# A hybrid scan and retrieval backbone: the adaLN modulation products dealt out anew over the stages

## The reference, cut to what matters

```python
silu_c, silu_cc = silu(c), silu(c_ctx)
for l in range(2):
    mod   = silu_c  @ w_mod[l] + b_mod[l]        # 6*1024 columns: sh1 sc1 g1 sh2 sc2 g2
    mod_c = silu_cc @ w_mod[l] + b_mod[l]
    proj  = (x * (1 + sc1) + sh1) @ w_in[l]      # scan input, z, pool, two gates
    y     = bidirectional_ssd(conv(proj))        # chunks of 128 tokens, 16 heads, 4 groups
    yg    = (y + d_skip * xh) * silu(z)
    yg    = yg * rsqrt(mean(yg * yg, over each of 4 groups) + eps)
    mix   = (sig(gp) * pool(proj) + sig(gs) * (yg * norm_g @ w_ssd_out)) @ w_o
    x     = layer_norm(ALPHA * x + g1 * mix)
    x     = layer_norm(ALPHA * x + g2 * peer(x * (1 + sc2) + sh2))
```

## Time and profile before

| | us |
|---|---|
| median of 3 runs (lowest, highest) | 4852.55 (4849.31, 4854.78) |
| the profiled execution's own time | 4852.04 |
| its span in the trace | 4850.2 |

### The profile page before, as it was taken

The page is one execution under the profiler, slowest core; times in us unless marked ns, Lnnn a source line. Parts: engine busy times, 40 slices in busy tenths (PEclk is TensorE's granted clock), DMA queues, the critical chain, the costliest instruction groups (busy, mean ns, idle before and its releaser), DMA issues. The chain is left out here.

```text
span 4850.2 us, 47618 instructions
## 1 busy us (share of the span) xinstructions
PE 3440.4 (71%) x15218; PEld 1720.0 (35%) x15218; DVE 3190.4 (66%) x6620; ACT 1537.8 (32%) x3751; POOL 2027.4 (42%) x1553
## 2 busy tenths in 40 slices
PE   7788889896778976555555557889897555555555
PEld 5576324332367433111111115777742111111111
DVE  5365787664465668776777756584566777777775
ACT  3442344343262235222222214362222222222221
POOL 0063444452023444555555550013345555555554
PEclk9889999998779998777777778979998777777777
DMA  5546999998633999999999991232299999999998
GB/s 198 207 144 260 410 418 410 423 423 365 255 115 128 380 418 401 403 420 417 411 417 422 415 418 51 81 103 78 104 374 407 418 413 420 413 412 419 416 416 362
DMA packets 263605, 1596.67 MB, mean 329 GB/s; under 512 B 43885, under 2 KB 50861, under 8 KB 77357
## 3 DMA queue, kind: packets, MB, share of 16 engines
q0 software_dynamic: 184320, 1342.26, 66.8%
q1 hardware_dynamic: 77738, 248.58, 14.2%
q10 hardware_dynamic: 1296, 2.79, 0.2%
HBM read 1575.86 MB, written 17.66 MB: 329 GB/s over the span
## 5 line engine op out<-in xcount | busy, mean ns | idle before, releaser
L2470 PE MATMUL banks<-arena 128*64 128x512 f32 x5120 | 1594.2, 759 | 1105.7 <-ACT arena L2293 1104.9
L2077 POOL DMA_INDIRECT arena<-in_experts,arena x1280 | 1497.9, 1170 | 1637.4 <-PE banks L2470 1375.7
L2163 DVE CUSTOM_DVE_ANT_0 arena<-arena,token_copies 128x1024 f32<-128x1024 f32 x1280 | 1637.0, 1297 | 669.0 <-DMA arena<-in_experts,arena 605.1
L2470 PEld LDWEIGHTS banks<-arena 128*64 128x64 f32 x5120 | 384.5, 166 | 2156.3 <-ACT arena L2293 1537.1
L2286 ACT ACTIVATE arena<-arena 128x2 f32<-128x2 f32 x640 | 131.2, 205 | 1776.7 <-DVE arena L2163 1767.4
L2293 ACT ACTIVATE arena<-arena 128x64 f32<-128x64 f32 x1280 | 376.0, 340 | 284.3 <-POOL arena L1948 243.7
L287 POOL TENSOR_TENSOR wide_low<-wide_blocks,wide_high 128x1024 fp32r<-128x1024 f32 x86 | 218.0, 2556 | 348.4 <-ACT wide_high L276 348.4
L924 POOL TENSOR_TENSOR arena<-arena 128x1024 f32<-128x1024 f32 x20 | 40.6, 2055 | 669.7 <-POOLq L807 610.0
L2349 PE MATMUL banks<-arena,wide_blocks 128*128 128x512 f32 (+3 forms) x960 | 311.7, 474 | 8.2 <-ACT arena L2192 6.7
L325 PE MATMUL banks<-activation_a,wide_high 128*128 128x512 f32 (+1 forms) x768 | 276.0, 359 | 8.4 <-ACT arena L349 2.7
L2422 PE MATMUL banks<-arena,wide_blocks 128*128 128x512 f32 x576 | 275.0, 615 | 0.0
(11 more groups left out here) (257 smaller groups left out, 4690.1 us busy)
## 6 DMA issues: line engine op xcount, KB each, us to landing
wide_blocks<-in_wide SPq DMA_DIRECT2D x168, 1024.0 KB
arena<-cum_rows SPq DMA_DIRECT2D x80, 256.0 KB, 3.2
arena<-in_experts,arena POOLq DMA_INDIRECT x1280
pre_scan<-arena SPq DMA_DIRECT2D x16, 256.0 KB
arena<-pre_scan SPq DMA_DIRECT2D x16, 256.0 KB, 9.3
residual<-in_tokens SPq DMA_DIRECT2D x6, 512.0 KB
arena<-mod_rows SPq DMA_DIRECT2D x6, 512.0 KB
norm_rows<-in_keys SPq DMA_DIRECT2D x3, 1024.0 KB
```

What stands on the lines that cost most here:

```text
L2077: pool.indirect_dma_start(out=v.ring[:, g % RING], out_offset=None, in_=io["experts"], in_offset=bass.IndirectOffsetOnAxis(ap=c.idx[:, u % ...
L2163: last = nc.vector.tensor_tensor_reduce(out=u_row, in0=u_row, in1=k.copies[:, n % NJ], scale=1.0, scalar=0.0, op0=ALU.mult, op1=ALU.add, a ...
L2470: mm = nc.tensor.matmul(k.ps[j * QUAD:(j + 1) * QUAD, a + half], v.lhs[:, g % 4, j], v.ring[:, (g * NJ + j) % RING, D + half * BANK:D + (h ...
```

## The change

- `stage_mods` computes its eight blocks by `more_mods`, in strips, with ACT as mover and the bias in PE's `combine`. It waits for the small tensor `pick` and one bias row first. It loads two of the six token tiles; the other four are loaded by the context's `stage_project`.
- `stage_states` for the context takes 12 blocks instead of 16; `stage_reload` takes none instead of 8; `stage_states` for the latent tokens of layer 0 takes 8 instead of 16, one behind each step instead of three. Its end doesn't wait for the stored rows.
- `stage_outputs` takes the other 20: 4 for the context, 8 and 8 for the latent tokens. One bank (7) serves them; every fourth unit PE combines the block before and multiplies the next; DVE moves parts and rows. SP loads a wide block before every fourth row from unit 12 on, loads three more after the last row, stores the mod rows and waits for them.
- The squared sums stay in `stage_outputs` only for the latent tokens of layer 0, and come two units later there. In the two other cases they move into `stage_merge`, behind the copies of the pool inputs; the square root follows them, and DVE's normalization moves behind the pooling.
- `stage_project` no longer rounds and cuts the merge's first block in layer 1; the merge does.

```diff
@@ stage_mods
+    mods = more_mods(k, 0, 0, brow, parts, 0, 1, n_blk)
...
-            load_wides(k, sp, WIDE_SLOTS)
-            for row in range(2):
-                sp.dma_start(brow[row:row + 1], io["b_mod"][:, 0, 0:2 * D]).then_inc(k.bias_loaded.sem, 16)
+            load_wides(k, sp, 2)
+            sp.dma_start(k.pick[:], io["pick"]).then_inc(k.bias_loaded.sem, 16)
+            mods.load(sp, 0)
+            load_wides(k, sp, n_blk)
...
-            for t in range(6):
-                load_wides(k, sp, WIDE_SLOTS + t)
+            for t in range(2):
                 sp.dma_start(k.res[:, t], io["tokens"][t]).then_inc(k.loaded.sem, 16)
             load_wides(k, sp, n_blk + WIDE_SLOTS)
-            sp.wait_ge(k.mod_used.sem, n_blk)
-            sp.dma_start(io["mods"][0, :, 0:2 * D], brow[0:2]).then_inc(k.mods_stored.sem, 16)
...
+            mods.keep(sp, 0)
+            mods.done(sp)
...
@@ more_mods
+    bank = (lambda i: 7) if alone else (lambda i: 6 + i % 2)
...
+        if alone and i >= 1:
+            pe.wait_ge(k.mod_used.sem, used0 + i)
@@ stage_project
-    last_cut = n_wide - 1 if layer == 0 else n_wide
+    last_cut = n_wide - 1
...
+            load_wides(k, sp, w0 + 6)
+            if stream == CONTEXT:
+                for t in range(2, 6):
+                    sp.dma_start(k.res[:, t], io["tokens"][t]).then_inc(k.late_tokens.sem, 16)
@@ stage_states
-                mods.done(sp)
...
-                for i in range(2 + 3 * n, 5 + 3 * n if n < len(steps) - 1 else mods.count + 1) if mods else ():
+                for i in range(2 + each * n, 2 + each * (n + 1) if n < len(steps) - 1 else mods.count + 1) if mods else ():
                     mods.multiply(pe, i)
@@ stage_outputs
+    turns = {4 * i: i for i in range(count)}
+    turns[len(units) - 1] = count
...
+            mods.load(sp, 0)
             for n, (t, d, g) in enumerate(units):
+                if n >= 12 and n % 4 == 0:
+                    load_wides(k, sp, w0 + n // 4 - 2 + WIDE_SLOTS)
...
+            load_wides(k, sp, w0 + count + WIDE_SLOTS)
+            mods.keep(sp, 0)
+            mods.done(sp)
...
+                if n in turns:
+                    i = turns[n]
+                    if i >= 1:
+                        mods.combine(pe, i - 1)
+                    mods.multiply(pe, i)
+                    if i == count:
+                        finish_used(k, pe)
                 intra(n)
...
-                if (d, g) == (1, 1) and t >= 1:
+                if squares_here and (d, g) == (1, GROUPS - 1) and t >= 1:
                     squares(t - 1)
-            squares(NT - 1)
+            if squares_here:
+                squares(NT - 1)
...
+                if n in turns and turns[n] >= 1:
+                    i = turns[n]
+                    mods.move(dve, nc.vector.tensor_copy, i - 1)
+                    if i >= 2:
+                        mods.copy_out(dve, nc.vector.tensor_copy, i - 2)
...
+            mods.copy_out(dve, nc.vector.tensor_copy, count - 1)
             add_y(NT - 1)
             gate(NT - 1)
@@ stage_merge
                 nc.scalar.copy(mixed[:, g, 0:T], k.ps[:, g % 2, 0:T]).then_inc(k.pin_copied.sem, 1)
+                if g < NT:
+                    squares(g)
+            nc.scalar.activation(rms[:, 0:NT], v.e32[:, 0:NT, 0:GROUPS], ACT.Sqrt, bias=k.eps[:],
+                                 scale=1.0 / GW).then_inc(k.rms_ready.sem, 1)
@@ build
-        w = stage_states(k, 0, CONTEXT, w)
-        stage_outputs(k, CONTEXT)
+        w = stage_states(k, 0, CONTEXT, w, mod_layer=0, first=8, count=12)
+        w = stage_outputs(k, CONTEXT, False, w, 0, 20, 4)
...
-        w = stage_reload(k, 0, w)
-        w = stage_states(k, 1, LATENT, w)
-        stage_outputs(k, LATENT)
+        stage_reload(k, 0)
+        w = stage_states(k, 0, LATENT, w, mod_layer=1, first=0, count=8)
+        w = stage_outputs(k, LATENT, True, w, 1, 8, 8)
...
-        stage_outputs(k, LATENT)
+        w = stage_outputs(k, LATENT, False, w, 1, 16, 8)
```

More of the change, by code:

```diff
@@ L393, in _ @@
             nc.scalar.activation(k.csil[:, :, 0:2], cvec, ACT.Silu).then_inc(k.h_ready.sem, 1)
+            for i in range(mods.count + 1):
+                mods.take(act, i)
         @block.gpsimd
@@ L787, in decay_steps, with stage_states @@
     return s
-def stage_states(k, layer, stream, w0=None, rows=True):
+def stage_states(k, layer, stream, w0=None, rows=True, mod_layer=0, first=0, count=0):
     nc, io = k.nc, k.io
@@ L804, in stage_states @@
              if ctx or o < NT - 1]
-    mods = more_mods(k, layer, 8, k.gates[:].rearrange("p a c -> p (a c)"), v.scr[:, 3 * D:3 * D + 512], w0, 1, 16) if w0 is not None else None
+    mods = more_mods(k, mod_layer, first, k.gates[:].rearrange("p a c -> p (a c)"), v.scr[:, 3 * D:3 * D + 512], w0, 1, count) if count else None
+    each = 3 if ctx else 1
     with nc.Block() as block:
@@ L1234, in _, with squares @@
         def _(act):
-            nc.scalar.activation(rms[:, 0:NT], v.e32[:, 0:NT, 0:GROUPS], ACT.Sqrt, bias=k.eps[:],
-                                 scale=1.0 / GW).then_inc(k.rms_ready.sem, 1)
+            def squares(t):
+                for g in range(GROUPS):
+                    nc.scalar.activation(sig[:, 0, 0:GW], v.zs[:, t, g * GW:(g + 1) * GW], ACT.Square,
+                                         accum_out=v.e32[:, t, g:g + 1])
+                    act.drain()
             round_wides(k, act, w0)
@@ L1390, in stage_merge, with stage_reload @@
     return w0 + n_wide
-def stage_reload(k, layer, w0):
+def stage_reload(k, layer):
     nc, io = k.nc, k.io
@@ L1436, in store @@
                 sp.dma_start(io["pre_part"][m], part[:, m % 2]).then_inc(k.part_kept[m % 2].sem, 16)
-            load_wides(k, sp, w0 + 6)
-            store(0)
-            store(1)
-            load_wides(k, sp, w0 + mods.count)
-            store(2)
-            store(3)
-            load_wides(k, sp, w0 + mods.count + WIDE_SLOTS)
-            mods.keep(sp, 0)
-            for m in range(4, 8):
+            for m in range(8):
                 store(m)
-            mods.done(sp)
             sp.wait_ge(k.reloaded[2].sem, C + 16 * (B_TILES + 8))
@@ L1500, in _ @@
             decay.logs(act)
-            for i in range(mods.count + 1):
-                mods.take(act, i)
-                if i == 5:
-                    decay.decays(act)
+            decay.decays(act)
         @block.vector
```

99 lines of the change are left out of this document (42 added, 57 removed).

## The result

The changed kernel takes 4802.85 us (median of 4 runs, 4801.87 to 4810.33) against 4852.47 (4849.31 to 4854.78): a ratio of 0.9901, 95% interval 0.9886 to 0.9917. Two repeats, each against new runs of the kernel before, gave 0.9908 (0.9892 to 0.9925) and 0.9911 (0.9896 to 0.9925). The profiled execution of the result is the 4810.33, the slowest of the four; its span is 4808.5.

| stage | before | forecast | after | repeats |
|---|---|---|---|---|
| first | 44.4 | 36 | 39.5 | 41.0, 39.3 |
| context: projection | 100.1 | no change | 98.4 | 99.2, 98.2 |
| context: states | 54.9 | 39 | 40.7 | 38.9, 40.7 |
| context: outputs | 47.7 | 46 | 55.1 | 55.2, 55.5 |
| context: merge | 143.8 | 146 | 143.4 | 142.8, 143.2 |

What follows compares the result with a forecast made beforehand. DMA was taken to bound the states stages with modulation blocks, PE the first stage, and PE, DVE and ACT together the outputs. Terms -8 - 15.8 - 9 - 31 + 7 + 3 = -53.8 from 4852.04 gave 4798 us, range 4783 to 4818.

Steps and rivals of the forecast that it cites:

- First stage, -8: First stage: falls from 44.36 to 36 us with blocks in strips; bounds -12 and 0.
- the rival of the slow short pieces: First stage and outputs: PE falls to its lower clock between short pieces, 4806 to 4816 us; chance 0.26.
- Context's states, -15.8: Context's states: four blocks fewer, 11.0 us, and no wait for the store's landing, about 4.8; range -14 to -16.5.
- Reload, -9: Reload: without blocks, DVE's waits for PE shrink from 11.8 to 2.5 us; bounds -6 and -11.
- Layer 0's states, -31: Latent tokens' states, layer 0: 32.3 us against 63.34, six steps of PE at 3.86; bounds -33.5 and -27.
- The +2 for a low clock at the start: Layer 0's states: 2 us added to 30.3 because PE's clock is low at the stage's start.
- Outputs, +7: Three outputs stages: layer 1 +3.5, layer 0 +5, context -1.5 with bounds -4 and +4.
- my signs: Outputs: lengths near 46, 90 and 90, PE's clock above 0.72; wrong if it falls below or a stage grows over 12.
- Merges, +3: Merges: context's +2 from normalization behind the pooling, layer 1's +1; bounds 0 and +8 for both.
- The tail of the outputs: End of outputs stages: waiting for the mod rows' store leaves about 2.5 us open, hidden behind the last squares in layer 0.
- that of PE's lower clock: First stage and outputs: short pieces run at PE's lower clock, giving 4806 to 4816 us; chance 0.26.
- the one in which the outputs cover everything: Three outputs stages: shrink by 4 + 1 + 4 us instead of growing by 7, giving 4782; chance 0.22.

Runs made afterwards that it cites:

- early: Changed kernel with two loads behind the first rows, first incoming-state products before unit 0 in all outputs, first stage's store ahead of its last load: 4801.18 us.
- best: As early, but incoming-state products come before the first unit only in the context's outputs: 4798.27 us.
- fill_rows: Changed kernel with late loads, early store, ACT moving parts and rows, and useless products filling PE's gaps in the context's outputs: 4799.25 us.

## Why the prediction was right, and where its steps were not

The forecast of 4798 was 4.9 us under the median of 4802.85, inside its range, and faster came out. That it came so close is partly luck: steps that gave too little and too much made up for each other, and the profile that is read below is the slowest run, 12 us above the forecast. Step by step:

- **First stage, -8: measured -3.3 to -5.1.** PE starts at 9.2, and the last five blocks come 2.8 us apart, both as reckoned. (The terms of the sum give 35.1, not 35.2.) Two terms failed. The first three blocks took 8.1 us, not 6: PE waited 0.54 us before the third and the fourth, for ACT's copy. And the store and its landing cost 7.5 us, not 5.1:

```profile
31.95 0.29 SPq L440 DMA_DIRECT2D mod_rows<-arena  x1
39.49 0.38 SPq L558 DMA_DIRECT2D arena<-mod_rows  x1
```

It stands behind the last 1 MB loads. The store ahead of the last of them, in `early`, shows that at most 1 us is to be had from its place in the queue, counted over this stage and the next. In the repeat with 41.0 PE waited 2.12 us for the last block, and its clock then fell, so that the last combination took 1.01 us a half instead of 0.59. The row was stored 3.8 us later than in the result and the stage ended 1.5 later; the rival of the slow short pieces has a part in that, and no run tells how much.
- **Context's states, -15.8: -14.2, -16.0, -14.2.** (179.4 + 3.4 + 0.3 + 0.4 is 183.5, 0.1 less than it says.) But the 4.8 us of landing counted as free were partly passed on: the wait at the end had also let the loads ahead land, and without it the next stage's first row stands behind them.
- **Reload, -9: -9.2 to -10.4.** DVE's wait for PE before its eight products is 2.5 us in the changed kernel, the 2.5 reckoned, and the wait before the sums' copy is gone.
- **Layer 0's states, -31: -32.9 to -33.0.** The step of PE is 3.86 us as reckoned: L876 at 1247.94, 1251.80, 1255.65, 1259.51. The +2 for a low clock at the start wasn't needed.
- **Outputs, +7: measured +16.7 in the result, +11.0 and +12.0 in the repeats.** Layer 1's: -0.2 to -0.9 where +3.5 was taken and -4 to +9 allowed. There the clock rose to 0.90 and PE's short pieces filled waits; of the 6.7 us that DVE got, its idle time took all. Each copy took 0.42 and 0.40 us, as costed (0.424 and 0.41). Layer 0's: +4.5 twice, +10.0 once, for +5. The **context's: +7.3 where -1.5 was taken and +4 was the bound**, and this is the step that failed. The runs split it: 2.5 are the late first row (55.1 to 52.6), 3.4 to 3.6 are the low clock (52.1 or 52.4 to 48.75; the same order in `early` and `best` differs by 4.1), and 2.7 remain to the 46 forecast. Of these, 2.2 can be seen at the end, in `fill_rows` as in the result, where the last combination stands ahead of the last head products at 0.50. No run takes it away.

```profile
226.61 1.01 PE L467 MATMUL banks<-arena,pick_stream 128*2 128x256 f32 x2
227.55 1.01 PE L468 MATMUL banks<-pooled_gates,ones 1*2 1x256 f32 x2
228.82 1.94 PE L963 MATMUL banks<-arena 128*128 128x64 f32 x8 [0.26 <-issue]
```

  The forecast said that ACT paces this stage. It nearly did before, with PE gapless beside it at 0.50 for its first units; with one block more in that stretch PE does, until its clock rises. Of my signs, a mean clock under 0.72 was reached here (0.71), and not in the latent stages (0.81, 0.90). For this stage it was a bad sign, since the clock was 0.64 before the change.
- **Merges, +3: -0.4 and +0.9.** The first L1376 comes 54.5 us after the merge's start, where the old L1341 came after 53.7: the normalization now stands in front of it, but by the second one DVE waits for PE again, and PE waits as long for these products as before (2.5 and 1.1 us in all):

```profile
281.94 6.30 DVE L1372 TENSOR_TENSOR arena<-arena 128x1024 f32<-128x1024 f32 x2
288.17 0.47 DVE L1376 SCALAR_TENSOR_TENSOR arena<-banks,arena 128x256 f32<-128x256 f32 x1
289.70 0.48 DVE L1376 SCALAR_TENSOR_TENSOR arena<-banks,arena 128x256 f32<-128x256 f32 x1 [1.07 <-PE banks L1225]
```

- **The tail of the outputs** was put at 2.5 us open; in the two stages without squares it is 0.3 and 0.7. In layer 1 the gate ends at 3191.8 (3190.53 + 1.23) and the next stage begins at 3192.47.

The terms in the result's own profile add up to -45.2 against -53.8: states and reload 1.7 better, first stage 3.1 worse, outputs 9.7 worse, merges 2.5 better. The rest, from -45.2 to the -41.7 of the spans, lies in stages that were put at nothing, 4.6 of it in the expert stages. Of the rivals, that of PE's lower clock came true in one stage of those it named, and now and then in part of another; the one in which the outputs cover everything came true in layer 1. As the two pull against each other, the forecast stood between them.

The Trainium skill (TensorE: Matmul & The Clock Gate, the section on HAM oscillation) says that PE loses its full rate in a loop whose wait for data is longer than the work between two waits. The context's outputs agree: their clock fell to 0.50 in a wait of 8.6 us behind 2 us of work. The first stage is another case, with waits of 0.5 to 1.0 us between pieces of about 2, and there the clock stayed at 1.00 from 10 to 30 us; the forecast's rival took the page too widely when it put the strips there at half rate.

## What to carry to other kernels

A wait at the end of a stage that looks like waste may be the time in which loads ahead land; when it goes, put the loads that the next stage needs first at the head of the queue, and the ones for later behind them. Work that is "hidden beside other engines" has its price at the clock that PE has just then: where a short stage opens with a wait of several us, as here, reckon its first units at the low clock. And look for the low clock in the instructions' own lengths, since no wait is noted for it.

## What was not expected of the hardware

The same instructions in the same order held the low clock for some 10 us in one kernel and for 30 in another (`early` and `best`), with PE busy 10.00 of 10 us in both; a third kept full clock for 30 us on useless work. What decides when it rises stays open, as does why layer 0's outputs fell back to 1.2 GHz at a wait of 0.92 us in six of twelve kernels and not in the other six. And more work for PE did not lengthen layer 1's outputs: the mean clock there went from 0.72 to 0.90 with it, and which of the two brought about the other no run shows.
